# A memory stage put in another order, with the sample tokens' matrix memories and the norms' factors computed on GpSimd

## The reference, cut to what matters

```python
C_new = a_c[..., None, None] * C + jnp.einsum('bshk,bshv->bhkv', kw, v)
n_new = a_c[..., None] * n + jnp.sum(kw, axis=1)
h = num / jnp.maximum(jnp.abs(nq), jnp.exp(-m_t))[..., None]
y = x * lax.rsqrt(jnp.mean(x * x, axis=-1, keepdims=True) + EPS)     # head_rmsnorm
```

## Time and profile before

| | us |
|---|---|
| three timed runs | 1849.45, 1852.45, 1852.46 (median 1852.45) |
| the profiled execution: its own time | 1849.23 |
| the profiled execution: span of the core | 1847.0 |
| TensorE busy in the span | 1687.7 (91%) |
| VectorE busy | 954.0 (52%) |
| ACT busy | 696.2 (38%) |
| GpSimd busy | 391.3 (21%) |
| mean granted clock of TensorE | 0.936 |

### The profile page before, as it was taken

One profiled execution on the slowest core, in us unless ns is written; L12 is line 12 of the kernel. 1 busy time (PEld: TensorE's weight loads), 2 busy tenths in 40 slices (PEclk: granted clock), 3 DMA queues, 4 the chain that ended last, 5 costly groups with the idle time before them and its releaser, 6 DMA issues.

```text
span 1847.0 us, 33779 instructions
## 1 busy us (share of the span) xinstructions
PE 1687.7 (91%) x13514; PEld 1625.7 (88%) x13514; DVE 954.0 (52%) x1433; ACT 696.2 (38%) x1050; POOL 391.3 (21%) x236
## 2 busy tenths in 40 slices
PE   6999978799999999998999877859999999999993
PEld 5999857789999999998998567859999999999993
DVE  5577676532210122226776765255746548457474
ACT  4533363342221223235333633443534435335342
POOL 4300250343443344443002503030000000000031
PEclk8999986699999999999999877969999999999997
DMA  4222227422222223222222212368778678677682
GB/s 176 81 70 77 74 72 266 188 80 92 92 87 86 81 92 105 79 81 69 69 77 78 70 50 86 112 211 277 241 246 288 217 255 290 216 266 259 234 313 75
DMA packets 71225, 271.42 MB, mean 147 GB/s; under 512 B 11668, under 2 KB 12404, under 8 KB 70300
## 3 DMA queue, kind: packets, MB, share of 16 engines
q1 hardware_dynamic: 63988, 250.52, 39.7%
q10 hardware_dynamic: 3464, 10.62, 1.8%
q0 software_dynamic: 3648, 8.53, 1.3%
HBM read 253.24 MB, written 36.34 MB: 157 GB/s over the span
## 4 chain that ended last, share of the span: by engine, by line
PE 81%; DVE 7%; POOL 4%; issue 3%; ACT 2%; DMA 1%; ACTq 0%; DVEq 0%; POOLq 0%; SPq 0%
PE psum L1189 39%; PE psum L1709 11%; PE psum L1719 10%; PE psum L1711 9%; PE psum L1236 9%; POOL r_cvt L674 2%; POOL r_w L676 1%; PE psum L1688 1%; PE psum L1241 1%; PE psum L1677 1%; DVE n L1780 1%; POOL r_cvt L675 1%; DVE r_bt L1964 0%; DVE acc L1767 0%; DMA wraw<-in_w_in 0%
## 5 line engine op out<-in xcount | busy, mean ns | idle before, releaser
L1709 PE MATMUL psum<-xg,xhi 128*128 128x320 f32 x1408 | 371.4, 307 | 1.2 <-issue 0.9
L1711 PE MATMUL psum<-xg,xlo 128*128 128x256 f32 x1408 | 369.7, 282 | 0.0
L637 POOL TENSOR_TENSOR wlo<-wraw,whi 128x1024 fp32r<-128x1024 f32 (+1 forms) x90 | 231.3, 2572 | 405.0 <-ACT whi L777 405.0
L1709 PEld LDWEIGHTS psum<-xg,xhi 128*128 128x128 f32 x1408 | 265.2, 188 | 3.5 <-issue 3.1
L1711 PEld LDWEIGHTS psum<-xg,xlo 128*128 128x128 f32 x1408 | 265.3, 188 | 0.0
L1189 PE MATMUL psum<-xnh,whi 128*128 128x260 f32 x1120 | 234.6, 291 | 32.1 <-POOL xnl L694 12.5
L777 ACT CAST whi<-wraw 128x1024 fp32r<-128x1024 f32 (+1 forms) x130 | 140.7, 1085 | 288.4 <-DMA wraw<-in_w_in 161.9
L415 DVE TENSOR_TENSOR xlo<-xraw,xhi 128x1024 fp32r<-128x1024 f32 x176 | 215.2, 1224 | 54.3 <-ACT xhi L1137 54.2
L1137 ACT CAST xhi<-xraw 128x1024 fp32r<-128x1024 f32 x176 | 182.7, 1048 | 142.1 <-PE psum L1711 142.0
L1189 PE MATMUL psum<-xnl,whi 128*128 128x260 f32 x1120 | 228.3, 286 | 0.0
L1189 PE MATMUL psum<-xnh,wlo 128*128 128x260 f32 x1120 | 228.2, 286 | 0.0
(11 more groups left out here) (427 smaller groups left out, 2422.1 us busy)
## 6 DMA issues: line engine op xcount, KB each, us to landing
xraw<-in_moe_gu SPq DMA_DIRECT2D x176, 512.0 KB, 4.2
xraw<-in_moe_dn SPq DMA_DIRECT2D x64, 704.0 KB, 5.8
wraw<-in_w_in SPq DMA_DIRECT2D x54, 512.0 KB, 3.2
wraw<-in_ffn_gu SPq DMA_DIRECT2D x44, 512.0 KB, 3.2
wraw<-in_ffn_dn SPq DMA_DIRECT2D x16, 704.0 KB, 4.1
wraw<-in_w_out SPq DMA_DIRECT2D x16, 512.0 KB, 3.5
out_cache_s<-in_cache SPq DMA_DIRECT2D x4, 2040.0 KB
rows_in<-in_zero SPq DMA_DIRECT2D x8, 640.0 KB, 33.8
```

What stands on the lines that cost most here:

```text
L637: pool.tensor_tensor(wlo[u % RAW][:, 0:cols], wraw[u % RAW][:, 0:cols], whi[u % SPL][:, 0:cols].bitcast(F32), ALU.subtract).then_inc(lo_ma ...
L1709: pe.matmul(epart(n), xhi[n % HIX][:, k * P:(k + 1) * P], xg[:, k, :], start=(k == 0), stop=False, skip_group_check=True)
L1711: ins = pe.matmul(epart(n)[:, 0:256], xlo[n % RWX][:, k * P:(k + 1) * P], xg[:, k, 0:256], start=False, stop=(k == KD - 1), skip_group_che ...
```

## The change

The matrix memories' update moves from VectorE to GpSimd: two products, the addition into the normaliser's column and the addition into the rest, started by VectorE's `c8_parts`; TensorE's `co` waits for `c8_made`. All norm factors of the memory stage, of the norm ahead of the experts and of the final norm are made by GpSimd as a multiply-add and a power of -0.5, instead of ACT's Ln and Exp. The final norm goes tile by tile.

VectorE's order in the memory stage is rewritten: weighted keys first, the HGRN sum of the sample tokens behind two of them, decayed scores later, two heads finished in a row. The decays `dw` move to other memory, and ACT's wait ahead of them goes. `wv` is done after `mt` 3 and in 16 matmuls instead of 24, from a wider `spw` with zeros. All eight `xnl` tiles are VectorE's, as is the low part of output unit 0; GpSimd makes those of units 1 and 2 in layer 0 and of the odd units in layer 1. The six state outputs are issued by SyncE, once `mt` 2 is made, in layer 0 behind the cache copies and zero fills.

```diff
-    jobs += [("wv",), ("mt", 3), ("fx",), ("mt", 4)]
+    jobs += [("mt", 3), ("wv",), ("fx",), ("mt", 4)]
...
-        spw, _ = at("spw", [P, 80])
+        spw, _ = at("spw", [P, 96])
+        nhalf, _ = at("nhalf", [P, 16])
...
-        R["dw"], o = at("r_dw", [P, 2, SEQ], F32, att_off)
-        R["qd"], o = at("r_qd", [P, 2, SEQ], F32, o)
+        R["dw"], o = at("r_dw", [P, 2, SEQ], F32, w0_end)
+        qd = [at("r_qd0", [P, SEQ], F32, o)[0], at("r_qd1", [P, SEQ], F32, att_off)[0]]
...
+                    if n == RAW - 1:
+                        made(sp, li, "mt", 2)
+                        for name, src in (("hgrn_p", R["sall"][:, NC - 1, :, :]), ("mlstm_p", R["call"][:, NC, :, :]),
+                                          ("hgrn_s", flat(TQ, 3 * NB * 64)), ("mlstm_s", flat(TSV, 3 * NB * 65)),
+                                          ("m_p", proj[0:5, 5, SEQ - 1:SEQ]), ("m_s", R["sc8"][0:5, 32:40])):
+                            sp.dma_start(a[name][li], src).then_inc(S("state_out"), 16)
...
+                C8 = flat(TSV, 3 * NB * 65).rearrange("p (n d) -> p n d", d=65)
+                vc = R["vc"][:].rearrange("p f (b d) -> p (f b) d", d=64)
+                ff, k8 = (R[k][:].rearrange("p f b -> p (f b)") for k in ("ff", "k8"))
+                pool.wait_ge(S("c8_parts"), 2 * li + 1)
+                pool.wait_ge(state_in, 64 * (li + 1))
+                step(pool.tensor_tensor(C8, C8, bc(k8.unsqueeze(2), P, 3 * NB, 65), ALU.mult))
+                step(pool.tensor_tensor(vc, vc, bc(ff.unsqueeze(2), P, 3 * NB, 64), ALU.mult))
+                step(pool.tensor_tensor(C8[:, :, 64], C8[:, :, 64], ff, ALU.add))
+                pool.tensor_tensor(C8[:, :, 0:64], C8[:, :, 0:64], vc, ALU.add).then_inc(S("c8_made"), 1)
+                for k, ss in enumerate((R["ss2"][:, 0:NC], R["ss2"][:], R["s10"][:], R["ss2"][:])):
+                    pool.wait_ge(S("ob_ms"), 4 * li + k + 1)
+                    step(pool.tensor_scalar(ss, ss, 1.0 / 64, EPS, ALU.mult, ALU.add))
+                    bump(pool.tensor_tensor(ss, ss, nhalf[0:ss.shape[0], 0:ss.shape[1]], ALU.pow), S("ob_rms"), pool)
...
                 if li == 0:
+                    pool.wait_ge(lo_made, los(U_OUT[0]) + 1)
+                    lo(U_OUT[0] + 1, KD * P)
+                    pool.wait_ge(mixl_dve, KD)
+                    lo(U_OUT[0] + 2, KD * P)
                 else:
-                    split_lo(pool, U_OUT[1], KD * P, lo_pool)
-                for m in range(0, KD, 2):
-                    pool.wait_ge(mixh_made, KD * li + m + 1)
-                    pool.tensor_tensor(xnl[:, m, :], proj[:, MIXT[m], :], xnh[:, m, :].bitcast(F32),
-                                       ALU.subtract).then_inc(mixl_pool, 1)
...
+            pool.wait_ge(S("squares_added"), 1)
+            step(pool.tensor_scalar(rms[:], rms[:], 1.0 / D, EPS, ALU.mult, ALU.add))
+            bump(pool.tensor_tensor(rms[:], rms[:], nhalf[:, 0:5], ALU.pow), S("rms_ready"), pool)
...
+            for t in range(5):
+                r = rms[0:tok(t), t:t + 1]
+                pool.wait_ge(S("last_squares"), t + 1)
+                step(pool.tensor_scalar(r, r, 1.0 / D, EPS, ALU.mult, ALU.add))
+                bump(pool.tensor_tensor(r, r, nhalf[0:tok(t), 0:1], ALU.pow), S("last_rms"), pool)
...
-            def head_rms(li, m):
-                act.wait_ge(S("ob_ms"), 3 * li + m - 1)
-                step(act.activation(R["ss2"][:], R["ss2"][:], ACT.Ln, scale=1.0 / 64, bias=K(C_EPS, 1)))
-                sig(act.activation(R["ss2"][:], R["ss2"][:], ACT.Exp, scale=-0.5), "ob_rms")
...
-                act.wait_ge(S("decode_made"), 3 * li + 2)
...
+                hi(U_OUT[li], KD * P)
+                act.wait_ge(S("ob_ms"), 4 * li + 4)
+                for n in range(1, SPL):
...
-                for name, src in (("hgrn_p", R["sall"][:, NC - 1, :, :]), ("mlstm_p", R["call"][:, NC, :, :]),
...
-                    act.dma_start(a[name][li], src).then_inc(S("state_out"), 16)
...
-                step(act.activation(yg[0:n, t, :], xtok[0:n, t, :], ACT.Square, accum_out=rms[0:n, t:t + 1]))
-            step(act.activation(rms[:], rms[:], ACT.Ln, scale=1.0 / D, bias=K(C_EPS, 1)))
-            sig(act.activation(rms[:], rms[:], ACT.Exp, scale=-0.5), "last_rms")
+                sig(act.activation(yg[0:n, t, :], xtok[0:n, t, :], ACT.Square, accum_out=rms[0:n, t:t + 1]), "last_squares")
...
+                    own = spw[0:80, 64:96].rearrange("p (g c) -> p g c", g=2)
+                    for b in range(NB):
+                        c = 2 * b
+                        j.mm(c, 2, R["cv"][:, b, 0, :], spw[:, c:c + 2])
+                        j.last = pe.matmul(j.out(16, 32).rearrange("p (g c) -> p g c", g=2)[:, :, c:c + 2],
+                                           R["cv"][0:80, b, 1, :], own[:, :, c:c + 2], start=True, stop=True,
+                                           skip_group_check=True)
...
-                pe.wait_ge(S("decode_made"), 3 * li + 3)
+                pe.wait_ge(S("c8_made"), li + 1)
+                pe.wait_ge(S("c8_parts"), 2 * li + 2)
                 query("co", R["qc8"], flat(TSV, 3 * NB * 65).rearrange("p (f b v) -> p f b v", f=3, b=NB), 65)
                 turn_heads(li, 2)
                 outputs((4,))
...
-                for b in range(NB):
-                    c = 2 * b
-                    j.mm(c, 2, R["cv"][:, b, 0, :], spw[:, c:c + 2])
-                    for g, (r, rows) in ((1, (0, 64)), (2, (64, 16))):
-                        j.mm(16 * g + c, 2, R["cv"][r:r + rows, b, 1, :], spw[r:r + rows, 64 + c:66 + c])
-                j.end()
                 turn_heads(li, 3)
+                values()
...
-                sig(tt(S8, S8, vb, ALU.add), "decode_made")
...
-                    step(v.tensor_copy(R["k8"][:], R["aw"][:, :, 0:NB]))
-                    v.wait_ge(state_in, 64 * (li + 1))
-                    step(tt(C8, C8, bc(k8, P, 3 * NB, 65), ALU.mult))
-                    step(tt(vc, vc, bc(ff, P, 3 * NB, 64), ALU.mult))
+                    sig(v.tensor_copy(R["k8"][:], R["aw"][:, :, 0:NB]), "c8_parts")
                     for f in range(3):
-                        step(tt(R["qc8"][:, f], bc(R["bt"][:, f, SEQ:T].unsqueeze(2), P, NB, NB),
-                                K(C_DM, NB * NB).rearrange("p (n m) -> p n m", m=NB), ALU.mult))
-                    step(tt(C8[:, :, 64], C8[:, :, 64], R["ff"][:].rearrange("p f b -> p (f b)"), ALU.add))
-                    sig(tt(C8[:, :, 0:64], C8[:, :, 0:64], vc, ALU.add), "decode_made")
+                        ins = tt(R["qc8"][:, f], bc(R["bt"][:, f, SEQ:T].unsqueeze(2), P, NB, NB),
+                                 K(C_DM, NB * NB).rearrange("p (n m) -> p n m", m=NB), ALU.mult)
+                        if f < 2:
+                            step(ins)
+                        else:
+                            sig(ins, "c8_parts")
...
-                decayed(0)
-                decayed(1)
                 weighted_keys(0)
                 weighted_keys(1)
+                sig(tt(S8, S8, vb, ALU.add), "decode_made")
                 running(0)
                 weighted_keys(2)
+                decayed(0)
                 running(1)
                 weighted_keys(3)
+                decayed(1)
                 running(2)
                 running(3)
                 s8_out()
                 c8_update()
+                made(v, li, "mo", 0)
+                decayed(2)
+                made(v, li, "mo", 1)
+                decayed(3)
                 finish(0)
+                finish(1)
                 mean_squares(li, 2)
-                finish(1)
-                decayed(2)
-                decayed(3)
+                finish(2)
                 normalise(li, 2)
-                finish(2)
-                mean_squares(li, 3)
                 finish(3)
                 decayed(4)
+                mean_squares(li, 3)
+                gate_heads(li, 2)
                 normalise(li, 3)
-                gate_heads(li, 2)
                 c8_out()
                 finish(4)
                 mean_squares(li, 4)
+                gate_heads(li, 3)
+                v.wait_ge(S("ob_rms"), 4 * li + 3)
+                sig(tt(R["obs"][:], R["obs"][:], bc(R["s10"][:].unsqueeze(2), NB, 10, 64), ALU.mult), "obs_normed")
+                split_lo(v, U_OUT[li], KD * P, lo_dve if li else lo_made)
+                normalise(li, 4)
...
-                gate_heads(li, 3)
-                v.wait_ge(S("obs_rms"), li + 1)
-                sig(tt(R["obs"][:], R["obs"][:], bc(R["s10"][:].unsqueeze(2), NB, 10, 64), ALU.mult), "obs_normed")
-                normalise(li, 4)
...
-                for m in range(1, KD, 2):
+                for m in range(KD):
```

More of the change, by code:

```diff
@@ L579, in _ @@
                         load(U_OUT[li] + n, a["w_out"][li, n], KD * P)
-                    if li == 1 and n == RAW - 1:
-                        sp.wait_ge(S("state_out"), 192)
```

(49 more changed lines are left out.)

27 lines of the change are left out of this document (10 added, 17 removed).

## The result

The changed kernel takes 1840.83 us (median of 5 runs, 1838.51 to 1842.97) against 1850.55 for the kernel before beside it: a ratio of 0.9949, with a 95% interval of 0.9933 to 0.9964. That is 9.7 us won where 20 were forecast. The profiled execution took 1840.83 us, its span 1839.0.

The account below looks back on a forecast made before the run. TensorE, last in the chain for four fifths of the span, was taken as the bound. Gains 6.6 + 11 + 0.9 + 1.5 = 20.0 off 1849.2 gave 1829.2; adding half of 3.2 gave 1831 us, range 1820 to 1845.

Parts of the forecast that it names:

- Sum: Whole kernel: gains of layer 0, layer 1, router and last norm, 6.6 + 11 + 0.9 + 1.5 = 20.0 us.
- three rivals: Layer 0 keeps whole gain: 1823, chance 0.18; VectorE pays for GpSimd: 1844, 0.18; GpSimd's matrix update bounds: 1862, 0.12.
- Layer 0: Layer 0's memory stage gains 14.7 us, of which 6.6 are kept after the wait for output projection unit 3.
- The first gap: TensorE's idle 6.77 us before the first state update in the memory stage: 4.3 won, 2.5 left.
- The cap: Layer 0's output projection: unit 3's weight load, queued behind fills and six outputs, lets unit 3 start only at 362.5.
- the rival built on it: Outputs and unit 3's load don't wait behind the fills; layer 0 keeps 14.7 instead of 6.6: 1823 us, chance 0.18.
- Layer 1: Layer 1's memory stage shrinks from 71.2 to 59.8 us, gain 11.4, taken as 11.
- Matrix update on GpSimd: Memory stage: GpSimd's update takes 10.9 us, hidden before the query; rival that it is the bound: 1862, chance 0.12.
- VectorE pays: Rival, memory stages: the 5.5 us taken off VectorE come back as waits at the port: 1844 us, chance 0.18.
- Power: GpSimd's norm factors: each multiply-add and each power on at most 10 elements takes 0.5 us.
- Router: VectorE's 0.92 us wait for ACT's Ln and Exp goes, hidden under VectorE's copies: gain 0.9 us.
- Last norm: Final norm tile by tile with GpSimd's factors: 9.0 us instead of 10.5, gain 1.5, ends -2 and 4.

Follow-up runs that it names:

- e6: Changed kernel with buffer addresses as in the kernel before and 31 instructions added at the start of TensorE's program: 1828.79 against 1848.93 us, ratio 0.9888.
- e4: Changed kernel with the six state outputs of each layer issued by ScalarE again: ratio 0.9972 to the kernel before.
- e7: Changed kernel with only the eight zero fills issued earlier, at about 237 us instead of 290: ratio 0.9911 to the kernel before.
- e9: Changed kernel, code place and addresses restored, zero fills early, with the matrix memories' four operations back on VectorE: 0.9819 of the kernel before (0.9828 without that move).
- e10: Changed kernel, code place and addresses restored, fills early, with three query tiles ahead of the copy releasing GpSimd: 0.9825 of the kernel before (0.9828 without).
- e11: Changed kernel, code place and addresses restored, fills early, with the heads' norm factors back on ScalarE: 0.9855 of the kernel before (0.9828 without).
- e1: Changed kernel with 15 more instructions (30 waits) at the start of TensorE's program: median 1841.17 us, ratio 0.9966 to the kernel before.
- e3: Changed kernel with the moved buffers back at their old addresses, no instruction differing: ratio 0.9930 to the kernel before.
- e5: Kernel before with 128 bytes left free behind spw, giving later buffers the changed kernel's addresses: ratio 1.0037 to the kernel before, 6.5 us slower.

## Why the prediction missed

The step that failed is the *Sum*: 20.0 taken off the profiled execution's own time, with the feed-forward part and the experts left at the lengths that they had, a term put at nothing without a reason. Its four terms came to 20.5 us in the trace, and 12.4 were lost where the prediction saw nothing to price: 6.1 at the second pass of the feed-forward loop and 6.3 in the experts. e6 takes both losses away and has the forecast gain. None of the three rivals was this. That 1840.83 lies within 1820 to 1845 is luck: the range was drawn for the sizes of the four terms and for the rivals.

The near agreement of 20.5 with 20.0, and of e6's 20.1, is in part luck too. In the profile of e6 layer 0 brings 3.5 us where 6.6 were forecast, and layer 1 with the router 14.3 where 11.9 were. The terms one by one, in the changed kernel:

- *Layer 0*, 6.6: 6.2 at the first feed-forward matmul. In the stage, two errors nearly cancel. The first gap left 3.8 us (0.46, 2.07, 1.23), not 2.5, and the waits for heads 5.5 (4.27, 1.25), not 1.6; the wv block took 3.7 us (321.47 to 325.22) instead of 11.31, most of it at the upper clock (0.98 granted from 321 to 325), where 3.8 off was forecast.
- *The cap*: the number was right (unit 3 at 363.1, forecast 362.5) and the reason half wrong. The last fill landed at 353.7, the last output at 358.5 and the load at 359.4, where 351.7, 356.1 and 358.8 were worked out (the 1.4 us to land had no row). But another queue for the six outputs wins nothing (e4), and with the fills gone the outputs hold nothing up: the fills, which the step named too, are the cap (e7). The rule in the Trainium skill, "DMA: Bandwidth & Descriptors", Issuing engines are not separate DMA queues, agrees with e4, where another engine's queue won nothing; the rival built on it expected that the load would therefore not be late, and it was.
- *Layer 1*, 11 (worked out 11.4): 13.1, as TensorE was busy for 43.8 us of the stage where 45.3 were worked out; the idle time, 14.3, was forecast at 14.5.
- *Matrix update on GpSimd*, 10.9: 9.0 (2.80, 2.76, 0.25, 3.15). It ended at 304.7, the query came at 313.36: hidden, as forecast. It is also worth nothing (e9): of the 5.5 us that VectorE was spared, 5.1 came back in the query tiles (5.81 against 0.74).
- *VectorE pays*: the wait is there (5.81 us for the query tiles against 0.74). It agrees with the rule in the Trainium skill, "SBUF — State Buffer", Who interferes with whom, that a VectorE instruction with two SBUF inputs contends with a GpSimd instruction that reads SBUF. The price is not there, since TensorE was busy without a gap from 293 to 324 (e10 takes the waiting away and wins nothing).
- *Power*, 0.5 each: 1.05 at 4, 1.65 at 8 and 1.94 at 10 elements per partition. That a factor on GpSimd still beats two tables on ScalarE is worth 5 us (e11).
- *Router*, 0.9: with what lies up to the first expert 0.8. *Last norm*, 1.5: 0.4. GpSimd's five pairs run one after another until 1829.62, and VectorE, which waited 4.41 us, still waits 3.80. By the code the first product needs only the first factor, which was there at 1824.4. VectorE is busy until 1826.5, then reads a flag and branches past passes that are not needed, until 1827.5. In all eleven kernels with this norm the first product starts 2.8 to 3.0 us behind that branch (3.4 in the kernel before, on ACT's factor), so the last factor, which the profile names, need not be what held it. No run separates the two.

Open: why an address moved by 128 bytes slows the 128x320 matmul, and why at the old addresses none to three of the seven steps are slow anyway, not the same ones each time. Which of the moved tiles matters was not tried, nor was TensorE's code moved in the kernel before.

## What to carry to other kernels

After a reordering, compare the stretches that the diff does not touch first: 31 instructions fewer ahead of a loop, and 128 bytes more among the tiles, cost some 6 us each in this kernel's trace, as much as the reordering won in layer 0. Try the change with the code's length and the addresses of the tiles restored before judging it. When a stage ends early, ask which background transfers (here zero fills, free to go 50 us earlier) were hidden by its old length.

## What the hardware showed unasked

- A loop of TensorE stands 2.2 to 3.5 us at the start of its second pass in the five kernels where it begins at the changed kernel's place or 15 instructions further (e1, e3, e4, e7 and the changed one), and not in the nine where it begins 30 or 31 further. In all five a 16 KB packet on the queue of instructions (q8) lands within the stand, 0.6 to 2.0 us behind its start, and TensorE goes on 1.4 to 1.6 us behind that landing. This suggests a wait for code; the trace doesn't say whose code the packet holds, so it is argued, not shown. In the changed kernel, the granted clock fell within the stand to the lower level (0.50, 1.2 GHz) and stayed there until 608.
- 128 bytes of address changed the mean of the same 128x320 matmul from 304 to 313 ns (e3 and the changed kernel) and from 306 to 313 (the kernel before and e5), at a granted clock of 1.00 each time.
- A small VectorE product of two SBUF tiles took 8 times as long (5.81 against 0.74 us for three) beside GpSimd's passes.
